# A trunk kernel on one core: its two families of triangular inverses cut down from 128x128 blocks to compact 64x64 tiles

## The reference, cut to what matters

```python
# layer 1, per head and chunk of 64 (layer 0's recurrence is brought to the same form)
kkt = einsum('bhncd,bhnsd->bhncs', k_beta, k) * decay
tri = where(strict, kkt, 0.0) + eye(64)
sol = triangular_solve(tri, rhs, lower=True, unit_diagonal=True)
```

## Time and profile before

| what | value |
|---|---|
| median of the three runs | 3313.81 us (3313.8 to 3314.01) |
| the profiled execution, its own time | 3316.79 us |
| its span, first to last instruction | 3315.1 us |
| mean granted TensorE clock | 0.987 |
| TensorE busy | 3180.3 us, 96% |
| TensorE's weight loads busy | 2933.4 us, 88% |
| VectorE busy | 1838.2 us, 55% |
| ScalarE busy | 1445.5 us, 44% |
| moved by DMA | 492.36 MB, mean 149 GB/s |

### The profile page before, as it was taken

The page is one execution under the profiler, slowest core; times in us unless marked ns, Lnnn a source line. Parts: engine busy times, 40 slices in busy tenths (PEclk is TensorE's granted clock), DMA queues, the critical chain, the costliest instruction groups (busy, mean ns, idle before and its releaser), DMA issues.

```text
span 3315.1 us, 57023 instructions
## 1 busy us (share of the span) xinstructions
PE 3180.3 (96%) x22180; PEld 2933.4 (88%) x22180; DVE 1838.2 (55%) x2397; ACT 1445.5 (44%) x2153; POOL 13.1 (0%) x28
## 2 busy tenths in 40 slices
PE   8999998989999999999999999999999999999997
PEld 8888887879898989889999998899987989899896
DVE  4555555575454554566556656565575655545455
ACT  4443333334343444434545545454454444434442
POOL 0000000000000000000000000000000000000000
PEclk9999999999999999999999999999999999999999
DMA  6333223445555565544333324443334555655553
GB/s 217 92 95 92 88 92 109 137 180 191 191 180 194 186 191 184 190 151 134 102 102 120 111 97 137 142 147 105 100 127 140 185 191 185 190 186 189 190 185 116
DMA packets 157019, 492.36 MB, mean 149 GB/s; under 512 B 15584, under 2 KB 50528, under 8 KB 155792
## 3 DMA queue, kind: packets, MB, share of 16 engines
q1 hardware_dynamic: 154032, 476.18, 44.2%
q0 software_dynamic: 2240, 12.07, 1.0%
q10 hardware_dynamic: 544, 1.05, 0.1%
HBM read 487.14 MB, written 2.10 MB: 148 GB/s over the span
## 4 chain that ended last, share of the span: by engine, by line
PE 83%; DVE 9%; ACT 4%; issue 3%; DVEq 0%; DMA 0%; ACTq 0%; SPq 0%
PE pp L390 68%; PE mb L704 3%; PE mb L718 3%; DVE wl L1231 2%; PE mb L698 2%; DVE ws L1572 1%; PE mb L540 1%; ACT wh L802 1%; PE mb L528 1%; PE mb L730 1%; PE mb L736 1%; PE mb L546 1%; PE mb L498 0%; DVE ws L1656 0%; ACT ws L1099 0%
## 5 line engine op out<-in xcount | busy, mean ns | idle before, releaser
L1231 DVE TENSOR_TENSOR wl<-raw,wh 128x1024 fp32r<-128x1024 f32 (+1 forms) x936 | 1101.4, 1185 | 889.2 <-ACT wh L802 880.0
L802 ACT CAST wh<-raw 128x1024 fp32r<-128x1024 f32 (+1 forms) x936 | 943.7, 1018 | 931.3 <-PE pp L390 930.6
L390 PE MATMUL pp<-aTh,wh 128*128 128x256 f32 x4400 | 1287.7, 293 | 41.0 <-DVE wl L1231 20.4
L390 PE MATMUL pp<-aTl,wh 128*128 128x256 f32 x4400 | 1251.6, 284 | 0.0
L390 PE MATMUL pp<-aTh,wl 128*128 128x256 f32 x4400 | 1251.5, 284 | 0.0
L390 PEld LDWEIGHTS pp<-aTh,wh 128*128 128x128 f32 x4400 | 850.1, 193 | 56.9 <-issue 28.5
L390 PEld LDWEIGHTS pp<-aTl,wh 128*128 128x128 f32 x4400 | 850.4, 193 | 4.4 <-issue 3.6
L390 PEld LDWEIGHTS pp<-aTh,wl 128*128 128x128 f32 x4400 | 849.4, 193 | 0.0
L390 PE MATMUL pp<-wh,hTh 128*128 128x512 f32 x1408 | 560.0, 398 | 17.3 <-DVE hTl L1602 7.8
L390 PE MATMUL pp<-wh,hTl 128*128 128x512 f32 x1408 | 551.0, 391 | 0.0
L390 PE MATMUL pp<-wl,hTh 128*128 128x512 f32 x1408 | 550.5, 391 | 0.0
(11 more groups left out here) (271 smaller groups left out, 2119.4 us busy)
## 6 DMA issues: line engine op xcount, KB each, us to landing
raw<-in_w_dram SPq DMA_DIRECT2D x800, 512.0 KB, 4.0
raw<-in_w_dram SPq DMA_DIRECT2D x136, 384.0 KB, 3.5
ws<-in_ln_dram POOLq DMA_DIRECT2D x8, 1024.0 KB, 7.7
out_dram<-xres SPq DMA_DIRECT2D x8, 256.0 KB, 2.0
ws<-in_lora_dram POOLq DMA_DIRECT2D x8, 192.0 KB, 2.6
xres<-in_x_dram ACTq DMA_DIRECT2D x2, 512.0 KB, 6.0
xres<-in_x_dram SPq DMA_DIRECT2D x2, 512.0 KB, 7.3
ws<-in_c_dram POOLq DMA_DIRECT2D x1, 832.0 KB, 8.1
```

The source lines that it names most:

```text
L390: last = mm(o, lhs, rhs, start=opens and m == 0, stop=end and kk == 1 and m == 2, skip_group_check=True)
L802: nc.scalar.copy(wh[:, q % RING, :, 0:width], raw[:, q, :, 0:width]).then_inc(S("hi_ready"), 1)
L1231: tt(wl[:, q % RING, :, 0:width], raw[:, q, :, 0:width], f(wh[:, q % RING, :, 0:width]), ALU.subtract).then_inc(S("lo_ready"), 1)
```

## The change

**Tiles.** All 64x64 matrices are stored compactly (64 columns, two chunks one above the other on the 128 partitions), and the products of the levels are made on quarters of the array: 64 rows by 64 columns, in the order of QUADS, so that neighbouring matmuls use other quarters. AX and dX have 32 moving columns in place of 64, and the VectorE operations on them half the elements. A block's one matmul becomes two. Transposes of X take two matrices side by side: 4 in `mix1` in place of 8, 2 in `mix0` in place of 4.

**Order.** A visit to an updated X first multiplies A by it, then transposes it. Each group of tiled matmuls has a `sem_inc` on TensorE's queue ahead of it (`to_tiles`), behind the waits of the group.

**mix1.** Levels 1 to 5 run on 64x64 tiles. The start is another: A^T is transposed on TensorE first (8 transposes), VectorE masks A from PSUM into the compact X. The sixth level joins the two halves: A21 times X (8 tiled matmuls of 64 columns), a negated copy, 8 tiled matmuls, a copy into X1; ScalarE copies the diagonal blocks into X1; then 8 transposes. The number of steps stays 30. The sigmoid's three activations move one level later, and VectorE's attention products and bound (1663, 1583) move behind levels 1 and 2.

**mix0.** The Gram products are 16 tiled matmuls with 128 columns and 8 more with 64 for A itself; VectorE makes X at once. AV, XAV and WT are 8 tiled matmuls each; AV goes behind the first dX. There is one step less (HOPS0 sums to 39): the steps with no half unit behind them are now 5 (the Gram products), 11 (third AX), 16 (fifth dX), 22 and 27.

```diff
-HOPS0 = (3, 4, 3, 3, 3) + 24 * (1,)
+HOPS0 = (3, 4, 3, 3, 3) + 23 * (1,)
...
+QUADS = ((0, 0), (1, 1), (0, 1), (1, 0))
...
-        X0 = r2(lay(4 * P), a=4)
-        XT0 = r2(lay(4 * P), a=4)
-        Yn0 = r2(lay(4 * 64), a=4)
+        X0 = r2(lay(4 * HC), a=4)
+        XT0 = lay(4 * HC).rearrange("p (h f c) -> p h f c", h=2, f=2)
+        Yn0 = r2(lay(4 * 32), a=4)
...
+            def to_tiles():
+                pe.sem_inc(S("tiles"), 1)
...
+                pe.wait_ge(S("sb_lo"), m1)
+                to_tiles()
                 for t in range(TT):
-                    for h in range(2):
-                        hr = slice(64 * h, 64 * h + 64)
-                        for w, src in enumerate((bt, kt_)):
-                            if t == 1 and h == 0 and w == 0:
-                                pe.wait_ge(S("sb_lo"), m1)
-                            last = mm(mb[2 * t + h][:, w * T:(w + 1) * T], src[hr, t * P:(t + 1) * P],
-                                      KR[hr, t, :, :], start=w == 0, stop=True, skip_group_check=True)
-                    last.then_inc(S("gram"), 1)
-                yield
-                pe.wait_ge(S("masked"), 2 * m + 1)
+                    for w, src in enumerate((bt, kt_)):
+                        for h, hf in QUADS:
+                            at = slice(t * P + HC * hf, t * P + HC * hf + HC)
+                            last = mm(mb[h][half(hf), (2 * t + w) * P:(2 * t + w + 1) * P], src[half(h), at],
+                                      KR[half(h), hf, :, t, :], start=t + w == 0, stop=True, skip_group_check=True)
+                last.then_inc(S("gram"), 1)
+                for t in range(TT):
+                    for h, hf in QUADS:
+                        at = slice(t * P + HC * hf, t * P + HC * hf + HC)
+                        last = mm(mb[2 + h][half(hf), t * HC:(t + 1) * HC], KR[half(h), hf, 0, t, :], bt[half(h), at],
+                                  start=t == 0, stop=True, skip_group_check=True)
+                last.then_inc(S("gram_a"), 1)
...
+                def transpose_x():
+                    for h in range(2):
+                        last = nc.tensor.transpose(mb[0][:, h * P:(h + 1) * P],
+                                                   X0[:, 2 * h:2 * h + 2, :].rearrange("p t c -> p (t c)"), ident)
+                    last.then_inc(S("Xnew"), 1)
+                def a_times_x(lv):
+                    for h in range(2):
+                        for hf, t in QUADS:
+                            Xp = X0[half(hf), 2 * h + t, :].rearrange("p (b w s) -> p b w s", w=2, s=1 << lv)
+                            last = mm(mb[2 + hf][half(t), h * T:h * T + 32], GM[half(hf), t, h, 0, 0, :], Xp[:, :, 0, :],
+                                      start=h == 0, stop=True, skip_group_check=True)
+                    last.then_inc(S("AX"), 1)
+                pe.wait_ge(S("X_ready"), 6 * m + 1)
                 pe.wait_ge(S("tok_ready"), m1)
-                for p in range(4):
-                    last = mm(mb[1][:, p * 64:(p + 1) * 64], GM[:, p // 2, p % 2, 1, 0, :],
-                              tok[:, 2, p // 2, 64 * (p % 2):64 * (p % 2) + 64], start=p == 0, stop=True,
-                              skip_group_check=True)
-                last.then_inc(S("AV"), 1)
-                yield
-                def a_times_x(lv):
-                    s = 1 << lv
-                    for p in range(4):
-                        Xp = X0[:, p, :].rearrange("p (b w s) -> p b w s", w=2, s=s)
-                        last = mm(mb[3][:, p * 64:(p + 1) * 64], GM[:, p // 2, p % 2, 0, 0, :], Xp[:, :, 0, :],
-                                  start=p == 0, stop=True, skip_group_check=True)
-                    last.then_inc(S("AX"), 1)
-                pe.wait_ge(S("X_ready"), 6 * m + 1)
+                to_tiles()
...
                 a_times_x(1)
+                transpose_x()
                 yield
                 for lv in range(1, 6):
                     pe.wait_ge(S("Yn"), 5 * m + lv)
-                    if lv > 1:
-                        pe.wait_ge(S("XT_ready"), 5 * m + lv - 1)
-                    for p in range(4):
-                        last = mm(mb[2][:, p * 64:(p + 1) * 64], XT0[:, p, :], Yn0[:, p, :], start=p == 0, stop=True,
+                    pe.wait_ge(S("XT_ready"), 6 * m + lv)
+                    to_tiles()
+                    for h in range(2):
+                        for t, hf in QUADS:
+                            last = mm(mb[t][half(hf), h * T:h * T + 32], XT0[half(t), h, hf, :], Yn0[half(t), 2 * hf + h, :],
+                                      start=h == 0, stop=True, skip_group_check=True)
+                    last.then_inc(S("dX"), 1)
+                    if lv == 1:
+                        for h in range(2):
+                            for hf, t in QUADS:
+                                last = mm(mb[2 + hf][half(t), h * T:h * T + HC], GM[half(hf), t, h, 1, 0, :],
+                                          tok[half(hf), 2, t, half(h)], start=h == 0, stop=True, skip_group_check=True)
+                        last.then_inc(S("AV"), 1)
+                    yield
+                    pe.wait_ge(S("X_ready"), 6 * m + lv + 1)
+                    if lv == 1:
+                        pe.wait_ge(S("AVs"), m1)
+                    if lv < 5:
+                        to_tiles()
+                        a_times_x(lv + 1)
+                    transpose_x()
...
+                pe.wait_ge(S("At"), g1)
+                for p in range(8):
+                    last = nc.tensor.transpose(mp[0][:, p * P:(p + 1) * P], At[:, p // 4, p % 4, :], ident)
+                last.then_inc(S("A1"), 1)
...
+                def a_times_x(lv):
+                    for h in range(4):
+                        for hf, c in QUADS:
+                            Xp = Xc[half(hf), 2 * h + c, :].rearrange("p (b w s) -> p b w s", w=2, s=1 << lv)
+                            last = mm(mb[hf][half(c), h * P:h * P + 32], At[half(hf), c, h, half(hf)], Xp[:, :, 0, :],
+                                      start=h == 0, stop=True, skip_group_check=True)
+                    last.then_inc(S("AX1"), 1)
...
+                for lv in range(1, 6):
                     pe.wait_ge(S("Yn1"), 6 * g + lv)
-                    if lv > 1:
-                        pe.wait_ge(S("XT1_ready"), 6 * g + lv - 1)
-                    for p in range(8):
-                        last = mm(mb[1][:, p * 64:(p + 1) * 64], XT1[:, p, :], Yn1[:, p, :], start=p == 0, stop=True,
-                                  skip_group_check=True)
+                    pe.wait_ge(S("XT1_ready"), 7 * g + lv)
+                    to_tiles()
+                    for h in range(4):
+                        for c, hf in QUADS:
+                            last = mm(mb[2 + c][half(hf), h * P:h * P + 32], XTc[half(c), h, hf, :], Yn1[half(c), 4 * hf + h, :],
+                                      start=h == 0, stop=True, skip_group_check=True)
                     last.then_inc(S("dX1"), 1)
                     yield
                     pe.wait_ge(S("X1_ready"), 7 * g + lv + 1)
-                    transpose_x(X1)
-                    if lv < 6:
+                    to_tiles()
+                    if lv < 5:
                         a_times_x(lv + 1)
-                    yield
+                    else:
+                        for h in range(4):
+                            for c in range(TT):
+                                last = mm(mb[0][half(c), h * HC:(h + 1) * HC], At[half(0), c, h, half(1)],
+                                          Xc[half(0), 2 * h + c, :], start=h == 0, stop=True, skip_group_check=True)
+                        last.then_inc(S("AX1"), 1)
+                    transpose_x()
+                    yield
+                pe.wait_ge(S("Yn1"), 6 * g1)
+                pe.wait_ge(S("XT1_ready"), 7 * g + 6)
+                to_tiles()
+                for h in range(4):
+                    for c in range(TT):
+                        last = mm(mb[2 + c][half(1), h * P:h * P + HC], XTc[half(c), h, 1, :], Y21[half(c), h, :],
+                                  start=h == 0, stop=True, skip_group_check=True)
+                last.then_inc(S("dX1"), 1)
+                yield
+                pe.wait_ge(S("X1_ready"), 7 * g1)
+                pe.wait_ge(S("X1_diag"), g1)
+                for p in range(8):
+                    last = nc.tensor.transpose(mp[1][:, p * P:(p + 1) * P], X1[:, p, :], ident)
+                last.then_inc(S("X1new"), 1)
...
+                    if lv < 6:
...
+                        nc.scalar.copy(XTc.rearrange("p h f c -> p (h f c)"), mb[2][:, :]).then_inc(S("XT1_ready"), 1)
...
+                    if lv == 3:
                         act.wait_ge(S("bounded"), 3 * g + 3)
                         st(go(SQ, SQ, ACT.Exp, scale=-1.0))
-                    elif lv == 3:
+                    elif lv == 4:
                         st.settle()
                         st(go(SQ, SQ, ACT.Ln, bias=1.0))
```

(77 more changed lines are left out.)

169 lines of the change are left out of this document (83 added, 86 removed).

## The result

The changed kernel takes 3183.28 us (median of 4 runs, 3182.32 to 3186.49), the kernel before 3313.83 (4 runs). The ratio is 0.9608 (95% interval 0.9591 to 0.9624), so it is 3.9% faster, 130.5 us. The prediction was 3182 (3145 to 3250). The profiled execution took 3186.5, with a span of 3184.8.

The account below looks back on a forecast made before the run. TensorE, busy for 96% of the span, was taken as the bound, with the inverses' work on the path. Gains of 86 us (mix1) and 46 (mix0) took 3316.8 to 3185; the median, 3.0 lower, gave 3182 us (3145 to 3250).

Parts of the forecast that it names:

- The sum: Whole kernel: 86 us gained in mix1 and 46 us in mix0 over eight groups, 132 us in all.
- What a tiled visit costs: Tiled products of the inverses: four waves 0.26 us, eight waves 0.49, plus costs of going to another shape and back.
- the low end: Cost of a tiled pair: 0.014 us, all four quarters overlapping, chosen from bounds of 0.014 and 0.057.
- The argument from two quarters to four: Tiled products: the earlier trace shows overlap in both directions, so four quarters were taken to overlap as two do.
- Two quarters at a time: Rival, tiled products: quarters on one half of the rows take turns, 0.029 a pair, 66 us back, 3246; chance 0.13.
- none: Rival, tiled groups: no quarters overlap, 0.057 a pair, 209 us back less some 35, 3356, slower; chance 0.05.
- the count behind levels 3 and 4: mix1: ScalarE has an activation ahead of the cast, X ready at t + 4.4, a wait of 0.45 each.
- the list of signs: Expected profile: mix1 waits about 1.6 before final transposes, 0.45 before third and fourth AX; mix0 waits 1.2 and 1.0.
- The handovers: The sem_inc ahead of each tiled group: costed at nothing, up to 0.22 us where no half unit covers it.
- the bound: Upper end for the sem_inc handovers: 24 visits x 8 groups x 0.22 = 42 us.
- The chain as the bound: Rival: ScalarE and VectorE chain sets the pace, 0.8 more per level, 50 us, about 3225; chance 0.10 with the handovers.
- the rival of 3450: Granted clock falls: the inverses' stages run at 1.2 GHz, half units alone add 270 us, about 3450; chance 0.03.

Follow-up runs that it names:

- the doubled product: Changed kernel with mix1's tiled product of A with X issued twice in each of its 5 visits a group: 3210.13 us, 24.6 us more.
- the last experiment: Kernel with ScalarE's side work and two half units moved, plus a half unit in each of mix0's two empty doubling-level visits: 3157.56 us, 15.7 more.

## Why the prediction was right, and where it was off

**The sum.** 132 us forecast, 130.5 measured; `mix1` 86 against 83.5, `mix0` 46 against 45.5. Both parts stand, `mix0`'s as a difference of two runs.

**What a tiled visit costs.** The choice of the low end, four quarters at once, decided the result, and the doubled product confirms it: 0.0146 a pair, predicted 0.014. From the last stream matmul ahead of dX to the second behind it are 1.03 us (1.07 forecast), around AX with its transposes 1.42 (1.50), a level 4.83 (4.95). The argument from two quarters to four, that both directions overlap in the trace before, came out right but was incomplete: the kernel taken quarter by quarter shows that it also needs the order in which the loops put the pairs. The change had them in turn.

**Two quarters at a time** (3246) would have made the doubled product cost 37 us, **none** (3356) 73; it cost 24.6, of which 18.7 are the product. (66 us on 3182 make 3248; the 3246 is a small slip.)

**mix1's waits.** Three of the four were named, with sizes too small. Behind two levels 0.45 was forecast, 0.60 and 0.59 were measured in the group shown. They stand before the fifth AX and the product of level 6, as the count behind levels 3 and 4 has it, and not before the third and fourth AX, where the list of signs puts them. Before the final transposes 1.6 was forecast, 2.17 measured; 0.3 of the difference is the two diagonal copies, 1.28 from the start of the first to the exponential, where 0.96 was counted. The wait before the first AX (0.89) was not named; the forecast only has a later start for that AX. The reason for the three later ones, ScalarE's side work ahead of the cast, is shown by moving it. The group's stage from its transposes of A came to 36.8 us (1625.18 to the last final transpose at about 1662.0) against 36.5: shorter levels and longer waits offset each other.

**mix0.** The waits before the operands' transposes (1.2 forecast, 1.18), before the last transpose of X (1.0, 0.9) and for the copy in level 3 (0.51) were where they were expected, and from line 529 to line 609 a group takes 22.5 us, 23.0 forecast. That gains 6.8 a group, but a whole group gains 5.5 from start to start (the operands' transposes of the second and third group start at 167.64 and 238.42 before, at 163.22 and 228.46 after). So outside that stage 1.3 was lost where 0.5 was forecast; 0.5 of it is line 501's new wait, and the rest is open. The two errors, 0.5 and 0.8 a group, run against each other, and so 45.5 stands closer to 46 than its terms do.

**The handovers.** Costing the increment at nothing is the term of the sum that the runs speak against. An extra one costs 0.05 to 0.07 us on average and 0.15 where a visit is bare, about 10 us in all if the first is paid like the next, which was not tested. If it is, other terms were as much too high, and the total came out by luck to that extent. The price stays under the 0.22 each, 42 us, of the bound. **The chain as the bound** (3225) was true in kind and smaller: 52 us of waits are in the kernel, but most of them were already in the sum.

**The clock** moved from 0.987 to 0.986 and decided nothing here; the rival of 3450 did not come. It does turn up in the last experiment.

**What the forecast did not ask** is whether multiplying A first helps. As the steps were filled, it cost 22 us; with the side work and two half units moved, the kernel takes 3141.8, 1.4% below the changed one and 5.2% below the kernel before, in either order.

## What to carry to other kernels

When many small products go to quarters of the array, let the innermost loop go over the quarters: the same instructions took 0.67 us in turn and 1.43 quarter by quarter. When a stage gets shorter, list what its other engines do in that step and move what nobody waits for behind the instruction that somebody does; that gave 30 us here with no work removed. Before you fill a visit that has no cover, look at what the step that gives up its work was covering: here the sum of the waits stayed the same, and the clock fell more often.

## What the runs showed that was not expected

- Eight pairs on one quarter and then eight on the next still overlap in part: 0.038 us a pair, not 0.057, though the starts within a quarter stay 0.058 apart.
- An extra semaphore increment on TensorE's queue ahead of a bare matmul costs 0.15 us (3.6 us for 24).
- Behind a wait of 3.2 to 3.3 us the stream ran on at half clock for a while in 6 groups of 7 (matmuls 0.21 to 0.22 apart); behind two waits of 1.34 and 0.56, or one of 2.45 and one of 0.56, in 4 of 7.
